# Stick-breaking heads between half units of the input projection, with logits and cumulative sums in one place in PSUM

## What is computed

```python
def even_mixer(h, w_in, conv_w, conv_b, w_a, b_a, w_x, b_x, lam, w_out):
    u = h @ w_in                                   # 1024 x 2560
    xr, gr, q, k, v = ...                          # 512 columns each
    xr = causal_dwconv(xr, conv_w, conv_b)         # width 4
    y_a = rglru(xr, w_a, b_a, w_x, b_x, lam) * gelu(gr)
    y_b = stick_breaking(q, k, v)                  # 8 heads of 64
    return concatenate([y_a, y_b]) @ w_out

def stick_breaking(q, k, v):                       # per head
    z = q @ k.T * 64 ** -0.5
    mask = key_pos < query_pos
    sp = where(mask, softplus(z), 0)
    log_w = log_sigmoid(z) - (reverse_cumsum(sp) - sp)
    return where(mask, exp(log_w), 0) @ v
```

## Time and profile before

| | |
|---|---|
| median of 3 runs | 1205.63 us (1205.12 to 1209.6) |
| profiled execution, first to last instruction | 1207.1 us |
| TensorE busy (its weight load) | 1170.7 us, 97% (975.9 us, 81%) |
| DVE busy | 708.3 us, 59% |
| ACT busy | 482.7 us, 40% |
| POOL busy | 73.6 us, 6% |
| DMA moved | 104.41 MB, mean 86 GB/s |
| chain that ended last, by engine | PE 87%, DVE 6%, ACT 4%, issue 1%, DMA 1% |

### The profile page before, as it was taken

How to read it: one execution, slowest core, us unless ns; L and a number is a source line. 1 busy time by engine, 2 the same in 40 slices (tenths; PEclk the granted TensorE clock), 3 DMA queues, 4 the chain that set the end, 5 groups by cost and what they waited for, 6 DMA issues and landing times.

```text
span 1207.1 us, 15133 instructions
## 1 busy us (share of the span) xinstructions
PE 1170.7 (97%) x5964; PEld 975.9 (81%) x5964; DVE 708.3 (59%) x848; ACT 482.7 (40%) x662; POOL 73.6 (6%) x53
## 2 busy tenths in 40 slices
PE   8999999999999999999999998899999999999997
PEld 7778755788888888888888787687788888899997
DVE  4758447248777766652226787438786667762222
ACT  4637357233444443342223318433544344432220
POOL 2000000033000000000111200032000000000000
PEclk9999979998999999999999999999999999999999
DMA  6323200031523332333332451041333233322331
GB/s 208 105 70 105 69 1 1 1 112 29 140 72 102 104 104 84 90 96 96 96 96 71 113 166 49 1 122 36 105 105 102 79 98 104 105 76 82 97 97 71
DMA packets 147478, 104.41 MB, mean 86 GB/s; under 512 B 4642, under 2 KB 144354, under 8 KB 147426
## 3 DMA queue, kind: packets, MB, share of 16 engines
q1 hardware_dynamic: 146466, 102.36, 28.6%
q10 hardware_dynamic: 960, 1.31, 0.5%
HBM read 98.02 MB, written 2.10 MB: 83 GB/s over the span
## 4 chain that ended last, share of the span: by engine, by line
PE 87%; DVE 6%; ACT 4%; issue 1%; DMA 1%; POOL 0%; POOLq 0%; SPq 0%; DVEq 0%; ACTq 0%
PE ps L1241 26%; PE ps L1243 26%; PE ps L1242 25%; PE ps L1417 2%; PE ps L1431 2%; DVE x L1034 2%; PE ps L1310 1%; ACT prob L749 1%; PE ps L1442 1%; ACT hx_hi L633 1%; DVE hx_lo L1038 1%; PE ps L1303 1%; DVE z_s L916 1%; DVE sp_lo L933 1%; PE ps L1315 1%
## 5 line engine op out<-in xcount | busy, mean ns | idle before, releaser
L1241 PE MATMUL ps<-hx_hi,w_hi 128*128 128x512 f32 x912 | 363.5, 399 | 2.8 <-DVE hx_lo L1038 1.9
L1242 PE MATMUL ps<-hx_lo,w_hi 128*128 128x512 f32 x912 | 357.6, 392 | 0.0
L1243 PE MATMUL ps<-hx_hi,w_lo 128*128 128x512 f32 x912 | 357.5, 392 | 0.0
L787 DVE TENSOR_TENSOR w_lo<-w_raw,w_hi 128x2048 fp32r<-128x2048 f32 (+1 forms) x90 | 201.6, 2240 | 170.2 <-ACT w_hi L507 170.2
L507 ACT ACTIVATE w_hi<-w_raw 128x2048 fp32r<-128x2048 f32 (+1 forms) x90 | 168.4, 1871 | 163.2 <-DMA w_raw<-in_ffn_w_down 115.5
L1241 PEld LDWEIGHTS ps<-hx_hi,w_hi 128*128 128x128 f32 x912 | 172.8, 189 | 43.8 <-DVE hx_lo L1038 4.9
L1242 PEld LDWEIGHTS ps<-hx_lo,w_hi 128*128 128x128 f32 x912 | 172.9, 190 | 37.0 <-issue 1.9
L1243 PEld LDWEIGHTS ps<-hx_hi,w_lo 128*128 128x128 f32 x912 | 172.6, 189 | 36.6
L1241 PE MATMUL ps<-w_hi,g_hi 128*128 128x256 f32 x352 | 99.4, 282 | 0.0
L1243 PE MATMUL ps<-w_hi,g_lo 128*128 128x256 f32 x352 | 99.1, 281 | 0.0
L1242 PE MATMUL ps<-w_lo,g_hi 128*128 128x256 f32 x352 | 99.1, 281 | 0.0
(11 more groups left out here) (193 smaller groups left out, 1564.6 us busy)
## 6 DMA issues: line engine op xcount, KB each, us to landing
w_raw<-in_ffn_w_up SPq DMA_DIRECT2D x88, 512.0 KB, 5.0
w_raw<-in_ffn_w_down SPq DMA_DIRECT2D x16, 1024.0 KB, 5.2
w_raw<-in_even_w_in SPq DMA_DIRECT2D x8, 1024.0 KB, 5.2
w_raw<-in_ffn_w_down SPq DMA_DIRECT2D x8, 768.0 KB, 4.7
w_raw<-in_odd_w_qkv SPq DMA_DIRECT2D x6, 1024.0 KB, 5.0
w_raw<-in_even_w_out SPq DMA_DIRECT2D x4, 1024.0 KB, 5.4
w_raw<-in_odd_w_o SPq DMA_DIRECT2D x4, 1024.0 KB, 6.0
x_in<-in_x SPq DMA_DIRECT2D x4, 512.0 KB, 6.6
```

The costliest lines, as they stand in the source:

```text
L787: dve.tensor_tensor(w_lo[s][:, 0:k], w_raw[s][:, 0:k], w_hi[s][:, 0:k], ALU.subtract).then_inc(w_lo_done, 1)
L1241: pe.matmul(dst, s_hi, r_hi, start=first, stop=False)
L1242: pe.matmul(dst, s_hi, r_lo, start=False, stop=False)
L1243: return pe.matmul(dst, s_lo, r_hi, start=False, stop=last)
```

## The change

It rewrites layer 0's mixer from unit 2 to the output projection.

- **Order of columns.** The units are now q, k, v, xr, xr, q, k, v, gr, gr; each first q, k or v unit holds what heads 0 to 3 need. A unit is done in two **halves** of one bank each (`half(n)`, n = 0 to 19), with a semaphore for each. Halves 4 and up take banks 6 and 7 in turn (4 and 5 take banks 4 and 5).
- **Heads between halves.** TensorE runs half(4), z(0), half(5), and then for each head h from 0 to 6: half(6+2h), z(h+1), cum(h), half(7+2h), av(h). At h = 3 the eight gate matmuls stand together ahead of half(12), and z(4) stands behind half(13). After that come parts of the output units over the products that are ready, with cum(7) and av(7) between them.
- **Logits stay in PSUM.** Head h has three banks (0 to 2 for even h, 3 to 5 for odd). The triangle and the ones are negated, and `sb_cum` accumulates onto the logits, so that DVE's copy (`sb_z`) and subtraction (`sb_t`) are gone; Abs, the DVE pass of softplus, and Exp read PSUM. `sb_av` writes into the first bank of the set once Exp has read it; `sb_out` is done for each head, on 64 partitions, and z(h+2) waits for it (`yb_ready`).
- **Keys zero-padded.** `kzs` holds a head's keys on their own 64 partitions and zeros on the other 64 (cleared by four memsets on POOL at the start), so that the logits' matmuls run over 128 rows. The mask and the identity are fp32r instead of bf16. One buffer each of `sp`, `sp_hi`, `sp_lo`, `z_s` instead of two, two, two and four.
- **The recurrent branch** moves to h = 0 to 7: taps at h = 0 and 1, gates at 3, square root at 4, scan at 5, GeLU at 7. The rotary angles, signs and sines move behind the last head.

The core of the diff (DVE's and ACT's heads, and TensorE's order):

```diff
-        order = [0, 256, 512, 768, 1024, 1280, 1536, 1792, 2048, 2304]
+        order = [1024, 1536, 2048, 0, 256, 1280, 1792, 2304, 512, 768]
...
         def sb_softplus(h):
...
-            act.wait_ge(z_copied, h + 1)
-            if h >= 2:
-                act.wait_ge(cum_mm, h - 1)
-            act.activation(sp[b][:], z_s[h % 4][:], ACT.Abs).then_inc(abs_done, 1)
+            act.wait_ge(z_mm, h + 1)
+            if h:
+                act.wait_ge(cum_mm, h)
+            act.activation(sp[:], z_of(h), ACT.Abs).then_inc(abs_done, 1)
...
+        for h in range(SB_HEADS):
+            if h:
+                sb_out(h - 1)
+            split_hi(h + 4)
+            if h == 7:
+                split_hi(h + 5)
+            if h in (0, 1):
+                center_tap(2 * h)
+            if h == 3:
+                lru_gates()
+            if h == 4:
+                act.wait_ge(lru_dve, 3)
+                act.activation(lru_th[:], lru_th[:], ACT.Sqrt).then_inc(lru_act, 1)
+                act.preload_act_table_set("natural_log_exp_and_others")
+            if h == 7:
+                act.wait_ge(half_evac, 2 * N_IN)
+                act.activation(gr[:], gr[:], ACT.Gelu_apprx_tanh).then_inc(lru_act, 1)
                 act.preload_act_table_set("natural_log_exp_and_others")
+            sb_weights(h)
+            if h + 1 < SB_HEADS:
+                sb_softplus(h + 1)
+            if h in (0, 1):
+                center_tap(2 * h + 1)
+            if h + 1 < SB_HEADS:
+                sb_hi(h + 1)
...
-        def sb_t(h):
-
-            dve.wait_ge(cum_mm, h + 1)
-            dve.tensor_tensor(z_s[h % 4][:], z_s[h % 4][:], bank(3, 3)[:, 0:SPAN], ALU.subtract).then_inc(t_done, 1)
...
+            if h < 7:
+                evac(6 + 2 * h)
...
             if h + 1 < SB_HEADS:
                 sb_softplus(h + 1)
+            if h < 7 and h != 3:
+                evac(7 + 2 * h)
             if h + 1 < SB_HEADS:
                 sb_lo(h + 1)
+            if h in (0, 1):
+                taps(2 * h + 1)
...
+        def sb_z(h):
+
+            if h in (0, 2, 4, 6):
+                pe.wait_ge(half_evac, {0: 3, 2: 4, 4: 13, 6: 14}[h])
+            if h == 1:
+                pe.wait_ge(half_evac, 6)
+            if h >= 2:
+                pe.wait_ge(yb_ready, h - 1)
+            for j in (0, 1, 3, 2):
+                dst = ps[:, T * sb_set(h) + OFF[j]:T * sb_set(h) + OFF[j] + T - P * j]
+                pe.matmul(dst, kzs[:, h % 4, P * j:P * j + P], qT[:, h // 2, P * j:T], start=j != 3, stop=False, skip_group_check=True)
+                last = pe.matmul(dst[:, 0:P], ident_r[:], mask_r[:], start=False, stop=False, skip_group_check=True)
...
+        def sb_av(h):
+            rows = slice(HD * (h % 2), HD * (h % 2) + HD)
+            pe.wait_ge(w_done, h + 1)
+            if h in (0, 4):
+                pe.wait_ge(half_evac, 6 if h == 0 else 16)
...
+        half(4)
         sb_z(0)
+        half(5)
+        for h in range(SB_HEADS - 1):
+            if h == 3:
+                lru_gates()
+            half(6 + 2 * h)
+            if h != 3:
+                sb_z(h + 1)
+            sb_cum(h)
+            half(7 + 2 * h)
+            if h == 3:
+                sb_z(h + 1)
+            sb_av(h)
+
+        ready = [4, 5, 6]
+        unit_ready(U_OUT[0])
+        pe.wait_ge(half_evac, 2 * N_IN)
+        pe.wait_ge(yb_ready, 6)
+        out_part(0, ready, first=True)
+        sb_cum(SB_HEADS - 1)
+        unit_ready(U_OUT[0] + 1)
+        pe.wait_ge(yb_ready, 7)
+        out_part(1, ready, first=True)
         sb_av(SB_HEADS - 1)
+        unit_ready(U_OUT[0] + 2)
+        out_part(2, ready, first=True)
+        pe.wait_ge(ya_ready, 1)
+        out_part(0, [0, 1, 2, 3])
+        pe.wait_ge(yb_ready, 8)
+        out_part(0, [7], end=True)
+        for j in (1, 2):
+            out_part(j, [0, 1, 2, 3, 7], end=True)
+        unit_ready(U_OUT[0] + 3)
+        out_part(3, range(UK), first=True, end=True)
```

More of the change, by code:

```diff
@@ new lines, in taps, with evac_gr @@
+        def taps(t):
+            dve.wait_ge(xc_center, t + 1)
+            for s in range(1, 4):
+                if s > 1:
+                    dve.wait_ge(xc_tap, 3 * t + s - 1)
+                dve.scalar_tensor_tensor(out=xc[:, t, s:], in0=(ug, uv)[t % 2][:, 0:T - s], scalar=col(V_CONV + 4 * (3 - s) + t),
+                                         in1=xc[:, t, s:], op0=ALU.mult, op1=ALU.add).then_inc(xc_tap, 1)
+        def evac_gr(n, t):
+            half_done(n)
+            dve.tensor_tensor(gr[:, t, :], bank(half_bank(n)), rbc[:], ALU.mult).then_inc(half_evac, 1)
@@ new lines, in sb_cum @@
+        def sb_cum(h):
+            pe.wait_ge(sp_lo_done, h + 1)
+            for j in range(TT):
+                for jj in range(j, TT):
+                    n = T - P * jj
+                    c0 = T * sb_set(h) + OFF[j] + P * (jj - j)
+                    for part in (sp_hi, sp_lo):
+                        last = pe.matmul(ps[:, c0:c0 + n], (tri_r if jj == j else ones_r)[:], part[:, OFF[jj]:OFF[jj] + n],
+                                         start=False, stop=(jj == TT - 1 and part is sp_lo), skip_group_check=True)
+            last.then_inc(cum_mm, 1)
@@ new lines, in sb_av @@
+        def sb_av(h):
+            rows = slice(HD * (h % 2), HD * (h % 2) + HD)
+            pe.wait_ge(w_done, h + 1)
+            if h in (0, 4):
+                pe.wait_ge(half_evac, 6 if h == 0 else 16)
+            for j in range(TT):
+                n = T - P * j
+                last = pe.matmul(bank(sb_set(h))[rows, P * j:T], v0[:, j, HD * h:HD * h + HD],
+                                 z_s[:, OFF[j]:OFF[j] + n], start=(j == 0), stop=(j == TT - 1))
+            last.then_inc(av_mm, 1)
@@ L1447, in _, with out_part @@
-        pe.wait_ge(group_evac, N_IN - 2)
+        def out_part(j, ks, first=False, end=False):
+            u = U_OUT[0] + j
+            for k in ks:
+                src = [(t[0][:, k, :] if k < LT else t[1][:, k - LT, :]) for t in ((ya_hi, yb_hi), (ya_lo, yb_lo))]
+                for b in range(2):
+                    last = three(bank(group_banks(N_IN + j) + b), *weights(u, k, b), *src, first and k == ks[0], end and k == ks[-1])
+                    if end and k == ks[-1] and b == 0:
+                        last.then_inc(m_first, 1)
+            if end:
+                last.then_inc(unit_done, 1)
```

463 lines of the change are left out of this document (212 added, 251 removed).

## The result

The changed kernel takes 1194.5 us (median of 4 executions, 1190.5 to 1196.8), the kernel before, in the same comparison, 1205.4 us (1203.2 to 1209.6). The ratio is 0.990 with a 95% interval of 0.988 to 0.993: faster by 10.9 us (0.9%), in the direction forecast and inside the range of 1182 to 1198, but 5.7 us above the forecast of 1188.8.

What follows compares the result with a forecast made beforehand. TensorE was taken as the bound from unit 2 to the output projection: 210.2 us of work - 7.8 for padding + 7.5 of waits = 209.9 against 226.7, so 16.8 off 1205.63 gives 1188.8 us; range 1182 to 1198.

Steps and rivals of the forecast that it cites:

- The sum of the stretch: Unit 2 to the end of the output projection: 209.9 us instead of 226.7, 16.8 us less.
- z 3.58 to 2.6, -7.8: Heads' logits blocks: padding keys to 128 rows shortens each from 3.58 to 2.6 us, 7.8 us less in all.
- Rival 1: Padding gains nothing, logits blocks stay at 3.58 us: gain 9.0, time 1196.6 us; chance 0.14.
- The clock, 9.0 us: Unit 2 to output projection: dense halves between heads' blocks keep TensorE's clock up, regaining 9.0 us.
- New waits, 7.5: TensorE waits at z(2), z(3), the gates, z(5) and av(4) in the new order: 7.5 us added.
- rival 3: Forecast waits too long, ACT and DVE being ahead: up to 7.5 us back, 1181 to 1186 us; chance 0.12.
- Work: TensorE's work from unit 2 to the output projection at full clock: 210.2 us before, less 7.8 for padding.
- Removed passes on DVE: Heads: dropping DVE's copy and subtraction, 16 passes of about 1.49 us, is worth only what leaves a chain.
- Covers: Moved rotary work beside the output matmuls costs nothing; unit 12's weights are just hidden, 18.5 against 19.0 us.
- the rest of the program is the same work in the same order: Outside unit 2 to the output projection nothing changes, so only the 16.8 us gain there counts.
- Rival 4: Clock falls at the gates and stays low; five heads so would give 1237 us, slower; chance 0.04.
- Rival 2: Clock falls in the gates' 2.9 us wait, costing 2 to 7 us: time 1191 to 1196; chance 0.20.

Runs made afterwards that it cites:

- keys_64: Changed kernel with only the padding undone: logits' matmuls read the 64 rows of their own head; 1211.9 us, ratio 1.005 to the kernel before.
- mask_bf16: Changed kernel with mask and identity in bf16 again, keys still padded; 1197.0 us, ratio 0.992 to the kernel before.
- no_wait_64: all_four with the logits' matmuls reading keys in 64 rows again; 1202.4 us, ratio 0.996 to the kernel before.
- copies_back: Changed kernel with DVE's two passes per head, copying the logits and their sum out of PSUM, put back; 1212.9 us, ratio 1.007 to the kernel before.
- all_four: Changed kernel with last output unit by bank, gates' sigmoid table load earlier, heads' outputs earlier, av(4) begun before its last v copy; 1184.2 us.
- last_by_bank: Changed kernel with only the last output unit done bank by bank, as before the change; 1190.0 us, ratio 0.989 to the kernel before.
- gates_late: Changed kernel with two more table loads on ACT ahead of the first sigmoid; 1199.5 us, ratio 0.994 to the kernel before.

## Why the prediction was right, and where not

**The sum of the stretch was right: 209.9 against 209.6**, but that is luck in part, since errors in it cancel. Its terms:

- *z 3.58 to 2.6, -7.8.* Measured 2.55, -8.2. Rival 1 is refuted by keys_64 and mask_bf16. The Trainium skill (TensorE: Matmul & The Clock Gate, LDWEIGHTS) says that the rows don't matter to a weight load, and the traces agree: 187 ns for one of 64 rows in keys_64, 191 ns for one of 128 rows in the changed kernel. But a z block of 64 rows is 1.3 us longer all the same. The drain that the same skill gives to a change of tiling mode (TensorEngine Tiling, Key Properties) would fit: from a mask to the next logits pass it is 0.26 us in keys_64 and 0.16 in the kernel before, and 0.06 over 128 rows in mask_bf16. No run here shows a drain itself.
- *The clock, 9.0 us.* Its size was right: 10.2 by windows in both profiles of before, 0 to 1.7 after. **The reason given was wrong.** The prediction took the dense halves between a head's blocks as what keeps the clock up. keys_64 and no_wait_64 have all these halves and lose 6.8 and 10.3 us, so the halves alone don't do it: in the new order the clock stays up only with the padding. The padding was costed at 7.8 us and is worth 16 to 18 in the new order (a part may be the fp32r masks', see keys_64), more than the whole gain of the change; without it the changed kernel is slower than the one before. Whether the padding alone would do it in the old order was not tried. The halves may still shorten a fall: the clock stayed low for 17 us at a stretch before, behind the 3.0 us wait, and for at most 6.8 in no_wait_64, but these two differ in more than the halves.
- *New waits, 7.5.* Measured 5.5: gates 2.66 (forecast 2.9), av(4) 1.67 (1.8), z(5) 0.78 (1.1), z(2) and z(3) 0.17 and 0.21 (0.7 each). The chains were right in place and order, each a little long; that is rival 3 in small, 2.0 us of its 7.5.
- *Work.* Forecast 202.4 us at full clock, measured 204.1. With each matmul counted from its start to the next one's, waits left out, the dense units and gates of the changed kernel take 75.1 us where 72.4 was taken, the two v units 23.3 where 22.8 was, and the heads' blocks with the output projection 105.6 where 107.2 was. The gate matmuls account for some 0.9 of the first: 0.98 us each (5.89 for six) where 0.86 was taken. Why the rest of the dense work takes longer isn't shown.
- *Removed passes on DVE.* "Worth only what they take out of a chain" stands, but no price was put on it. copies_back gives one: the new order without the removal would have lost 12.4 us more in waits and 6.8 in clock. The interleaving lives on it.
- *Covers.* Single buffers, the moved rotary work and unit 12's weights cost nothing, as forecast: TensorE's waits in the stretch name none of them, and all_four has no wait at all.

**The step that failed is the sentence "the rest of the program is the same work in the same order".** The last output unit was written in another order, which the prediction had in its diff (`out_part(3, range(UK), first=True, end=True)` where `unit` had stood) and did not follow to the semaphore `m_first`. A wait of 1.4 us came of it, and low clock behind that: 5.0 us in the profiles, of the 5.7 by which the forecast was off (two profiles of each kernel, of which one of before had low clock there too). last_by_bank takes it out, and its 1190.0 us lie 1.2 above the forecast. The last 0.7 us are open.

**Rival 4's sum** was wrong as it stands in the prediction. By its own rule, one us more for each us of full-speed work done at half clock, the gain of 16.8 us is used up within one head with its halves (18.8), not within two, and five heads would give 1188.8 + 94 = some 1283 us, not 1237. Nothing of the kind was seen.

**The median.** Taking the gain read from one profile off the median of the runs was sound for the stretch, since it is the same in both profiles of before (226.7 and 227.0). The boundary is not: it differs by 2.2 us between them.

**Rival 2** (the clock falls in the gates' wait) happened in 3 of the 6 profiles that have the 2.7 us wait and in none without it, and cost 1.7 us each time, less than the 2 to 7 forecast. It cost 3.4 with 5.2 us of wait (gates_late), and as much in copies_back, with 3.2 us behind another of 1.2.

## What to carry to other kernels

When a loop over two indices is turned inside out, look for signals that count on the old order: half a unit's lead of one bank was worth 3 to 4.6 us here, more by the clock it kept up than by the wait. Price a short wait of TensorE, or a block of matmuls over half the rows, together with the low clock that may follow, and look for it in several profiles, since it falls in some and not in others. A pass that is hidden in one order can be the bound in the next, so cost a removal against the order it makes possible.

## What the runs showed of the hardware that was not expected

- The granted clock fell from 2.4 to 1.2 GHz with TensorE busy throughout, behind blocks of four fp32 matmuls over 64 rows with a 128-row mask matmul after each (no_wait_64: five times, 10.3 us lost, no wait). The same blocks over 128 rows brought it down in no profile without a wait right ahead of the block (all_four: no fall; copies_back: two, behind 4.3 and 2.3 us). What in the block does it, the rows or the gaps between its matmuls, was not tried.
- A mask matmul in fp32r behind a 64-row matmul takes 0.33 us, the one in bf16 took 0.23: the z block with 64 rows is 3.87 us with the one, 3.58 with the other. Over 128 rows the type made no difference (2.55 and 2.52).
- The start of the program varies too. In 2 of 14 profiles unit 2 began at 38.7 to 39.0 us, in the others at 42.3 to 43.5. TensorE early in last_by_bank:

```profile
7.16 4.66 PE L1354 MATMUL ps<-ones_r 128*128 128x128 f32 x32
```

The same instructions and what follows in the changed kernel:

```profile
7.08 7.07 PE L1354 MATMUL ps<-ones_r 128*128 128x128 f32 x32
...
15.24 0.63 PE L1286 MATMUL ps<-hx_lo,w_hi 128*128 128x512 f32 x1
```

The slower start shows matmuls at half pace (0.63 us for 128x512) up to 17.8 us (up to some 19 in all_four and keys_64), though the PEclk of that window reads 1.00, so the losses of the table don't hold it. Four microseconds of difference between two profiles can come from there, which is why stages were compared here and not spans.
